# Rounded three-product attention scores in a hybrid encoder step on one NeuronCore

## The reference, cut to what matters

```python
def select_and_attend(q, qi, wi, q_pos, k_all, v_all, ki_all, k_pos, topk):
    ...
    top_val, top_idx = lax.top_k(score, topk)
    ...
    logits = jnp.einsum('btngd,btknd->btngk', qg, kg).astype(jnp.float32) * (HEAD_DIM ** -0.5)
    logits = jnp.where(valid[:, :, None, None, :], logits, -jnp.inf)
    p = jax.nn.softmax(logits, axis=-1).astype(vg.dtype)
    o = jnp.einsum('btngk,btknd->btngd', p, vg)
```

## Time and profile before

| | before |
|---|---|
| median of 3 runs | 3011.31 us (3008.76 to 3017.05) |
| profiled execution, its own time | 3008.23 us |
| span of the profile | 3006.5 us |
| TensorE busy (matmuls) | 2856.5 us, 95% |
| VectorE busy | 1643.6 us, 55% |
| ScalarE busy | 987.3 us, 33% |
| GpSimd busy | 648.8 us, 22% |
| mean granted TensorE clock | 0.985 |

### The profile page before, as it was taken

How to read it: one execution, slowest core, us unless ns; L and a number is a source line. 1 busy time by engine, 2 the same in 40 slices (tenths; PEclk the granted TensorE clock), 3 DMA queues, 4 the chain that set the end, 5 groups by cost and what they waited for, 6 DMA issues and landing times.

```text
span 3006.5 us, 43059 instructions
## 1 busy us (share of the span) xinstructions
PE 2856.5 (95%) x16186; PEld 2453.2 (82%) x16186; DVE 1643.6 (55%) x2804; ACT 987.3 (33%) x1260; POOL 648.8 (22%) x280
## 2 busy tenths in 40 slices
PE   5999889999999999999989989899999999999997
PEld 2778733379999999999977876234999999999996
DVE  7758777785452534524544777763435344344355
ACT  4246646533221111111233565563332111121112
POOL 2411410011222222222242034000112212222221
PEclk9999999999999999999999999999999999999999
DMA  5412100242222222212241311002112222222222
GB/s 218 138 64 85 37 22 1 57 162 84 84 84 70 84 70 84 86 54 85 76 135 47 123 43 37 1 1 64 43 64 91 64 76 80 73 84 72 82 83 86
DMA packets 71352, 224.95 MB, mean 75 GB/s; under 512 B 17232, under 2 KB 17488, under 8 KB 70096
## 3 DMA queue, kind: packets, MB, share of 16 engines
q1 hardware_dynamic: 70192, 219.36, 21.7%
q10 hardware_dynamic: 1056, 4.19, 0.3%
HBM read 211.44 MB, written 11.54 MB: 74 GB/s over the span
## 4 chain that ended last, share of the span: by engine, by line
PE 42%; issue 32%; DVE 11%; ACT 7%; POOL 4%; DVEq 2%; DMA 1%; ACTq 0%; POOLq 0%; SPq 0%
PE ps L980 33%; ACT notsel L779 5%; POOL w_lo L617 4%; PE ps L1238 2%; DVE smax L1732 1%; PE ps L1222 1%; PE ps L1031 1%; DVE hf L1389 1%; DMA w_ada<-in_w_ada 1%; PE ps L1226 1%; PE ps L1206 1%; DVE s_cand L1519 1%; DVE s_keep L1531 1%; PE ps L1228 1%; PE ps L1094 1%
## 5 line engine op out<-in xcount | busy, mean ns | idle before, releaser
L617 POOL TENSOR_TENSOR w_lo<-w_raw,w_hi 128x1024 fp32r<-128x1024 f32 x202 | 500.4, 2477 | 1852.8 <-ACT w_hi L730 1852.8
L980 PE MATMUL ps<-u_hi,w_hi 128*128 128x352 f32 (+1 forms) x2112 | 457.5, 325 | 2.1 <-ACT rstd L931 2.1
L980 PE MATMUL ps<-u_hi,w_lo 128*128 128x352 f32 (+1 forms) x2112 | 458.4, 325 | 0.0
L980 PE MATMUL ps<-u_lo,w_hi 128*128 128x352 f32 (+1 forms) x2112 | 455.6, 324 | 0.0
L730 ACT CAST w_hi<-w_raw 128x1024 fp32r<-128x1024 f32 x202 | 211.0, 1045 | 528.4 <-PE ps L980 337.7
L980 PEld LDWEIGHTS ps<-u_hi,w_hi 128*128 128x128 f32 x2112 | 362.1, 189 | 3.7 <-ACT rstd L931 2.7
L980 PEld LDWEIGHTS ps<-u_lo,w_hi 128*128 128x128 f32 x2112 | 361.0, 189 | 0.0
L980 PEld LDWEIGHTS ps<-u_hi,w_lo 128*128 128x128 f32 x2112 | 360.9, 189 | 0.0
L779 ACT ACTIVATE notsel<-score,s_cand 128x384 bf16<-128x384 f32 (+3 forms) x248 | 297.5, 1200 | 139.3 <-DVE s_cand L1519 139.1
L1830 DVE SCALAR_TENSOR_TENSOR x<-ps,mod,x 128x704 f32 (+2 forms) x240 | 125.5, 579 | 347.5 <-PE ps L980 341.1
L980 PE MATMUL ps<-a_hi,w_hi 128*128 128x352 f32 x1056 | 228.7, 325 | 4.3 <-POOL w_lo L617 2.1
(11 more groups left out here) (265 smaller groups left out, 4152.5 us busy)
## 6 DMA issues: line engine op xcount, KB each, us to landing
w_ada<-in_w_ada SPq DMA_DIRECT2D x96, 512.0 KB, 4.8
w_raw<-in_w_up SPq DMA_DIRECT2D x88, 512.0 KB, 3.4
w_raw<-in_w_in SPq DMA_DIRECT2D x34, 512.0 KB, 3.5
cw<-in_convw SPq DMA_DIRECT2D x32, 512.0 KB, 5.1
ada_later<-in_w_ada SPq DMA_DIRECT2D x24, 512.0 KB, 3.6
w_raw<-in_w_down SPq DMA_DIRECT2D x32, 384.0 KB, 3.1
w_raw<-in_w_down SPq DMA_DIRECT2D x32, 320.0 KB, 2.9
w_raw<-in_w_out SPq DMA_DIRECT2D x16, 512.0 KB, 3.5
```

The lines of the kernel that those rows point to most:

```text
L617: nc.gpsimd.tensor_tensor(w_lo[slot][:], w_raw[:], w_hi[slot][:].bitcast(F32), ALU.subtract)\
L980: last = nc.tensor.matmul(ps[:, bank + t, 0:w], wt[slot][:, kk, :], mv[:, kk, t * TW:t * TW + w], start=(at == 0 and p == 0), stop=(at == ...
```

## The change

For blocks 2 to 7 the scores are made of three rounded products. ScalarE rounds the keys of each head (`k_two`, its own 64 rows) and the queries of each block (`q_two`), GpSimd computes the rests (`k_lo`, and `q_lo`, written over `q`), and SyncE copies within SBUF: the low key part of a head goes to the other 64 rows of `k_two`, the high query part is doubled. One product on 128 rows then gives q_hi k_hi + q_hi k_lo; a second on 64 rows adds q_lo k_hi. Blocks 0 and 1 and the sampled tokens keep the full products.

```diff
+        k_lo = place("k_lo", PT_O + 4608, [P, SEQ], F32R)
+        k_two = [place(f"k_two{n}", PT_O + 4608 + 4096 * (1 + n), [P, SEQ], F32R) for n in range(2)]
+        q_two = {i: place(f"q_two{i}", off, [P, 2, 4, P], F32R) for i, off in
+                 [(2, PT_O + 4608 + 3 * 4096), (3, PT_O)] + [(i, X_O + 4 * TILE + (i - 4) * 4096) for i in range(4, QB)]}
...
+        q_lo = place("q_lo", R_O, [P, 4, TOK], F32R)
...
+                def double_queries(i):
+
+                    sp.wait_ge(q_high.sem, q_high.at(l, i - 1))
+                    settle(sp)
+                    sp.dma_start(q_two[i][64:128, 0].bitcast(F32), q_two[i][0:64, 0].bitcast(F32)).then_inc(q_doubled[i].sem, 16)
+                    sp.dma_start(q_two[i][0:64, 1].bitcast(F32), q_two[i][64:128, 1].bitcast(F32)).then_inc(q_doubled[i].sem, 16)
+
+                double_queries(2)
+                double_queries(3)
+                sp.wait_ge(k_low.sem, k_low.at(l, 1))
+                settle(sp)
+                sp.dma_start(k_two[0][64:128, :].bitcast(F32), k_lo[0:64, :].bitcast(F32)).then_inc(k_doubled.sem, 16)
+                sp.dma_start(k_two[1][0:64, :].bitcast(F32), k_lo[64:128, :].bitcast(F32)).then_inc(k_doubled.sem, 16)
+                for i in range(4, QB):
+                    double_queries(i)
                 sp.wait_ge(gated.sem, gated.at(l, 2))
...
                 sp.wait_ge(c_ready.sem, c_ready.at(l, 2))
+                sp.wait_ge(pv_used.sem, pv_used.at(l, N_S))
...
-                for m in range(2):
+                def gate(m):
                     pool.wait_ge(sp_taken.sem, sp_taken.at(l, m + 1))
                     nc.gpsimd.tensor_tensor(mix[:, m, :], mix[:, m, :], gu[:, m, :], ALU.mult).then_inc(gated.sem, 1)
 
+                def queries_low(i):
+                    pool.wait_ge(q_high.sem, q_high.at(l, i - 1))
+                    at = slice(i * P, (i + 1) * P)
+                    pool.drain()
+                    for n in range(2):
+                        r = slice(64 * n, 64 * n + 64)
+                        last = nc.gpsimd.tensor_tensor(q_lo[r, :, at], q[r, :, at], q_two[i][r, n].bitcast(F32), ALU.subtract)
+                    last.then_inc(q_low.sem, 1)
+                    pool.drain()
+
+                gate(0)
+                pool.wait_ge(k_high.sem, k_high.at(l, 1))
+                pool.drain()
+                for n in range(2):
+                    r = slice(64 * n, 64 * n + 64)
+                    last = nc.gpsimd.tensor_tensor(k_lo[r, :], k[r, 0:SEQ], k_two[n][r, :].bitcast(F32), ALU.subtract)
+                last.then_inc(k_low.sem, 1)
+                queries_low(2)
+                gate(1)
+                for i in range(3, QB):
+                    queries_low(i)
...
+                def queries_high(i):
+
+                    for n in range(2):
+                        r = slice(64 * n, 64 * n + 64)
+                        last = nc.scalar.copy(q_two[i][r, n], q[r, :, i * P:(i + 1) * P])
+                    last.then_inc(q_high.sem, 1)
+
+                act.wait_ge(kv_rot.sem, kv_rot.at(l, 5))
+                for n in range(2):
+                    r = slice(64 * n, 64 * n + 64)
+                    last = nc.scalar.copy(k_two[n][r, :], k[r, 0:SEQ])
+                last.then_inc(k_high.sem, 1)
+                queries_high(2)
+                act.wait_ge(sp_ready.sem, sp_ready.at(l, 2))
+                queries_high(3)
                 act.wait_ge(vaug_ones.sem, vaug_ones.at(l, 1))
...
+                act.drain()
+                for i in range(4, QB):
+                    queries_high(i)
                 nc.scalar.preload_act_table_set(LN_EXP)
...
+                def rounded(i):
+
+                    if i == SEARCHED[0]:
+                        pe.wait_ge(k_doubled.sem, k_doubled.at(l, 32))
+                    pe.wait_ge(q_doubled[i].sem, q_doubled[i].at(l, 32))
+                    pe.wait_ge(q_low.sem, q_low.at(l, i - 1))
+                    settle(pe)
...
+                    if i in SEARCHED:
+                        if (b, c) == (0, 0):
+                            rounded(i)
+                        for n in range(2):
+                            nc.tensor.matmul(ps[:, bank + n, 0:w], q_two[i][:, n, b, :], k_two[n][:, c:c + w], start=True, stop=False)
+                        for n in range(2):
+                            nc.tensor.matmul(ps[:, bank + n, 0:w], neg_ident[:, 0, :], selection(i, c, w), start=False, stop=False)
+                        for n in range(2):
+                            r = slice(64 * n, 64 * n + 64)
+                            last = nc.tensor.matmul(ps[:, bank + n, 0:w], q_lo[r, b, i * P:(i + 1) * P], k_two[n][r, c:c + w],
+                                                    start=False, stop=True)
...
                     for n in range(2):
-                        nc.tensor.matmul(ps[:, bank + n, :], k[64 * n:64 * n + 64, kb * P:(kb + 1) * P],
-                                         q[64 * n:64 * n + 64, :, i * P:(i + 1) * P], start=True, stop=False)
+                        r = slice(64 * n, 64 * n + 64)
+                        if i in SEARCHED:
+                            nc.tensor.matmul(ps[:, bank + n, :], k_two[n][:, keys], q_two[i][:, n, :, :], start=True, stop=False)
+                        else:
+                            nc.tensor.matmul(ps[:, bank + n, :], k[r, keys], q[r, :, queries], start=True, stop=False)
...
+                    if i in SEARCHED:
+                        for n in range(2):
+                            r = slice(64 * n, 64 * n + 64)
+                            last = nc.tensor.matmul(ps[:, bank + n, :], k_two[n][r, keys], q_lo[r, :, queries], start=False, stop=True)
                     last.then_inc(st_ready.sem, 1)
```

More of the change, by code:

```diff
@@ L177, in build @@
         vnat = place("vnat", PT_O, [P, QB + 1, P], F32)
+        k_lo = place("k_lo", PT_O + 4608, [P, SEQ], F32R)
+        k_two = [place(f"k_two{n}", PT_O + 4608 + 4096 * (1 + n), [P, SEQ], F32R) for n in range(2)]
+        q_two = {i: place(f"q_two{i}", off, [P, 2, 4, P], F32R) for i, off in
+                 [(2, PT_O + 4608 + 3 * 4096), (3, PT_O)] + [(i, X_O + 4 * TILE + (i - 4) * 4096) for i in range(4, QB)]}
+        assert PT_O + 4608 + 4 * 4096 <= RING_O
         gv = place("gv", X_O, [P, 2, TOK], F32)
@@ L382, in build @@
         sp_taken = signal("sp_taken", 2)
+        k_high = signal("k_high", 1)
+        k_low = signal("k_low", 1)
+        k_doubled = signal("k_doubled", 2 * DMA)
+        q_high = signal("q_high", len(SEARCHED))
+        q_low = signal("q_low", len(SEARCHED))
+        q_doubled = {i: signal(f"q_doubled{i}", 2 * DMA) for i in SEARCHED}
         v_turned = signal("v_turned", 1)
@@ L1204, in logits @@
                         pe.wait_ge(sel_ready.sem, sel_ready.at(l, SEARCHED.index(i) + 1))
-                    for n in range(2):
-                        nc.tensor.matmul(ps[:, bank + n, 0:w], q[64 * n:64 * n + 64, b, i * P:(i + 1) * P],
-                                         k[64 * n:64 * n + 64, c:c + w], start=True, stop=False)
-                    m0 = c if i in SEARCHED else i * P
-                    for n in range(2):
-                        last = nc.tensor.matmul(ps[:, bank + n, m0 - c:w], neg_ident[:, 0, :], selection(i, m0, c + w - m0),
-                                                start=False, stop=True)
+                    if i in SEARCHED:
[11 more added lines that the diff above has]
+                        for n in range(2):
+                            nc.tensor.matmul(ps[:, bank + n, 0:w], q[64 * n:64 * n + 64, b, i * P:(i + 1) * P],
+                                             k[64 * n:64 * n + 64, c:c + w], start=True, stop=False)
+                        m0 = i * P
+                        for n in range(2):
+                            last = nc.tensor.matmul(ps[:, bank + n, m0 - c:w], neg_ident[:, 0, :], selection(i, m0, c + w - m0),
+                                                    start=False, stop=True)
                     last.then_inc(s_ready.sem, 1)
@@ L1220, in st @@
                     bank = PLACE["S", t]
+                    keys, queries = slice(kb * P, (kb + 1) * P), slice(i * P, (i + 1) * P)
                     for n in range(2):
-                        nc.tensor.matmul(ps[:, bank + n, :], k[64 * n:64 * n + 64, kb * P:(kb + 1) * P],
-                                         q[64 * n:64 * n + 64, :, i * P:(i + 1) * P], start=True, stop=False)
+                        r = slice(64 * n, 64 * n + 64)
+                        if i in SEARCHED:
+                            nc.tensor.matmul(ps[:, bank + n, :], k_two[n][:, keys], q_two[i][:, n, :, :], start=True, stop=False)
+                        else:
+                            nc.tensor.matmul(ps[:, bank + n, :], k[r, keys], q[r, :, queries], start=True, stop=False)
                     if masked(i, kb):
@@ L1227, in st @@
                     for n in range(2):
```

(7 more changed lines are left out.)

## The result

The changed kernel takes 3032.11 us (median of 4 runs, 3028.92 to 3032.49). The kernel before, run beside it, takes 3013.55 (4 runs, 3008.76 to 3017.05). The ratio is 1.0069, with a 95% interval of [1.0048, 1.0091]: slower by 18.6 us between these medians, where I had forecast 16. The profiled execution took 3031.93 us.

What follows compares the result with a forecast made beforehand. VectorE's chain was taken to bound the attention's head and middle, TensorE its end. GpSimd's +21.0 less the products' 5.4, with preparation free, gave +15.6 on 3011.3: 3027 us, range 3010 to 3040.

Steps and rivals of the forecast that it cites:

- What bounds the kernel: Attention: VectorE's chain sets the head (387.4 to 401.5 us) and middle (to 486), TensorE's time counts at the end (to 614).
- The products, -5.4 us: TensorE's score units: 27 on the path per layer gain 0.10 us each, 2.7 us a layer, 5.4 in both.
- The preparation, 0: ScalarE's key and query copies and SyncE's transfers fall into existing waits or are hidden; nothing charged.
- GpSimd, +21 us: Head: GpSimd's rests and second gate alternate with VectorE's two-input operations, delaying its chain 10.5 us a layer, 21 in both.
- my 4 to 12.4: Range of GpSimd's delay per layer: about 4 if VectorE keeps its place, 12.4 if the diagonal comes after the gate.
- the 10.8 us of its work without cover: Head: GpSimd's 15.1 us of work less 4.3 in which it moves for free; the rest stands before VectorE operations.
- its alternative of 9.3: Head: GpSimd's delay per layer in us if VectorE's three one-input operations don't wait and run beside.
- Low pair one after the other: Rival, score units: one-pass products on 64 rows do not run side by side; +11.5 us more, 3038; chance 0.12.
- The lock bites little: Rival, head: GpSimd delays VectorE only 4 us a layer; +3 in all, 3014, no measurable change; chance 0.15.
- Faster: Rival: GpSimd is done or VectorE goes first, and row-mode changes cost nothing extra; 3001 us; chance 0.08.
- I am wrong if: L(2) before 405 us, S unit under 3.6 or over 3.8, or TensorE waiting for k_doubled, q_doubled or ScalarE's copies at L(2).

Runs made afterwards that it cites:

- f_gate_fill: e_gate plus bf16 products nobody reads (fillers) in TensorE's waits before last score units of blocks 4 to 7 and block 7's first value product; 3011.69 us, ratio 1.0001.
- h_after_fill: The changed kernel plus the same unread filler products in the same TensorE waits as f_gate_fill; 3022.37 us, ratio 1.0038.
- g_before_fill: The kernel before plus the same unread filler products in the same places as f_gate_fill, as its control; 3007.36 us, ratio 0.9990.
- b_no_rests: The changed kernel without GpSimd's fourteen k_lo and q_lo operations, TensorE doing the same number and kinds of products; 3019.43 us, ratio 1.0029.
- a_old_products: The changed kernel with the old full products for blocks 2 to 7, all rests, copies, transfers and waits kept; 3024.68 us, ratio 1.0046.
- c_later: The changed kernel with the second gate held until block 1's first score unit, rests of blocks 3 to 7 until the previous block's; 3021.36 us, ratio 1.0033.
- e_gate: c_later with the second gate moved on to the first score unit of block 2, ahead of the rest of block 3; 3022.53 us, ratio 1.0035.
- j_stack_fill: f_gate_fill with four products on 128 rows for blocks 4 to 7 (query low parts doubled) and more fillers; 3005.33 us, ratio 0.9986.

## Why the prediction was right

The time, 3027 against 3032, and the direction were right, but the closeness is luck: of the two terms one was too large and the other had the wrong sign, and they made up for each other.

**What bounds the kernel.** Right. The loss sits in the head, the middle stage hardly moved (from L(2) to S(4) 84.0 to 83.9 us in layer 0, 84.1 to 85.5 in layer 1), and the end is TensorE's.

**The products, -5.4 us.** This step failed. The unit was nearly right: 3.71 us against 3.68, a gain of 0.07 instead of 0.10, made of 0.21 of columns saved and 0.14 of longer changes (0.51 beside the columns now, 0.37 before), where I had 0.13. Two things were wrong behind it. First, 27 times this gain does not reach the end: at full clock, where f_gate_fill and h_after_fill show it, S(4) to the end takes 0.5 us less than with the old products and the same fillers (126.9 to 127.0 against 127.4), since the waits for VectorE's maxima and output take up the rest: in layer 0 TensorE is busy for 1.4 us less than in g_before_fill (123.1 against 124.6) and idle for 1.0 more (3.8 against 2.8). Second, I held the clock to be the one of before. It isn't: with the cheaper products TensorE runs at half clock behind waits that the kernel before passes at full clock, and each such stretch costs about 2 us in the last stage (96.4 against 94.2 with one, 98.1 to 98.4 with two). Without GpSimd's share the change costs 9 us (b_no_rests; 11.3 by its stages). On top of GpSimd's delay the products add 7.4 us by the time, of which 2.7 are in the stages (changed kernel less a_old_products), so no run fixes their price: behind which waits the clock falls differs from run to run. I had used the clock for the head only.

**The preparation, 0.** Right: ScalarE's first exponential still waits for TensorE, 8.50 us, and no product waits for a transfer or a copy. b_no_rests keeps all of it and L(2) starts on time.

**GpSimd, +21 us.** The mechanism was right in its detail, and the size was off: 7.6 us a layer, 15.3 in both, and 14 by a_old_products, inside my 4 to 12.4. GpSimd had the gate and ten operations left when VectorE's chain began, as predicted. What I took for granted was that the 10.8 us of its work without cover all stand in front of VectorE. The rows show that VectorE also moves while GpSimd waits its turn (the gate took 3.24 us instead of 2.42, the pair at 411.37 2.85 instead of 2.58) and in its pauses of 0.16 to 0.24 us, and a VectorE operation waits only for what is left of GpSimd's, not for all of it. The one-input operations waited in part: the pair of L1614 took 1.83 us instead of 0.82, L1674 0.58 instead of 0.42. My sum had assumed that they wait, its alternative of 9.3 that they don't.

**The rivals.** *Low pair one after the other:* no, the pair is busy for 0.49 us and not 0.63; but the next product begins 0.43 us after it, so its saving was not there either. *The lock bites little:* no, 7.6 and not 4. *Faster:* no. None of them held the clock.

**The points of "I am wrong if".** L(2) at 413, where I had said 412. That hit is luck too: it is 21.8 us behind L(0), where I had 24.6, and L(0) happened to begin 4.1 us later. S unit 3.71, no wait for `k_doubled` or `q_doubled`. All held, and none would have shown the clock: I had listed unit times at full clock, not the granted clock of the windows in the end stage.

**Left open.** Why the stage from L(2) to S(4) varies between 83.3 and 88.5 us, even between the layers of one execution. It goes with where its half-clock stretches fall, but no run separates cause from effect there.

## What to carry to other kernels

Work that is moved to an idle GpSimd is not free if it reads SBUF beside a chain of small VectorE operations: each of them may wait for the rest of one GpSimd instruction, so hang such work on a signal that falls where VectorE reads PSUM or waits. When TensorE's products get cheaper in a part where it also waits, read the granted clock behind each wait, before and after. A few unread products in the wait can be worth more than the saving (here some 9 us, 3 of which the old kernel gains too, against 1 us that the products save from S(4) on), so try them on the old kernel as well. And one-pass products on half the rows may cost more in changes of rows than they save in columns: here a unit of four products on 128 rows takes 3.56 us, one with the third on 64 rows 3.71.

## What was not expected of the hardware

- A wait of 1.48 us behind full float32 products left the clock at 1.00; one of 1.59 us behind the cheaper form was followed by half clock and cost about 2 us. It is no fixed length that decides: c_later passed a wait of 1.58 us at the same product (560.90) at full clock, in both layers, and fell to half behind the next one, of 1.84 us. Layer 0 of e_gate passed both at full clock. What decides between them stays open. With 1.04 us of fillers in such a wait and 0.62 us left idle (h_after_fill) the clock stayed at 1.00.
- A change between 128 and 64 rows around a one-pass pair on 64 rows costs about 0.18 us here, as much as one weight load of 189 ns, and 0.11 around a full one, in a stream where the other products show only 0.15 us beside their columns per unit.
- The third product on 64 rows, side by side for the two heads, takes nearly as long until the next product (0.43 us) as two in a row on 128 rows (0.46, 604.42 to 604.88 in j_stack_fill).
- A memset on GpSimd leaves VectorE's two-input operations alone (0.15 us), and stretches a one-input TENSOR_SCALAR (1.28 instead of 0.82 us).
